# Order of the q and k products in the level stage of a hybrid decoder block, and the place of its operand region

## What is computed

```
b = jnp.cumsum(gi, axis=-2)
decay = jnp.where(causal, jnp.exp(jnp.where(causal, diff, 0.0)), 0.0)   # diff = b_i - b_j
attn = jnp.einsum('bhid,bhjd,bhijd->bhij', qi, ki, decay)
intra = jnp.einsum('bhij,bhje->bhie', attn, vi)
```

## Time and profile before

| | us |
|---|---|
| median of 3 runs | 1651.62 |
| lowest, highest | 1650.98, 1652.35 |
| the profiled execution, its own time | 1652.26 |
| its span, first to last instruction | 1650.5 |

### The profile page before, as it was taken

How to read it: one execution, slowest core, us unless ns; L and a number is a source line. 1 busy time by engine, 2 the same in 40 slices (tenths; PEclk the granted TensorE clock), 3 DMA queues, 4 the chain that set the end, 5 groups by cost and what they waited for, 6 DMA issues and landing times.

```text
span 1650.5 us, 29297 instructions
## 1 busy us (share of the span) xinstructions
PE 1622.8 (98%) x11680; PEld 1520.2 (92%) x11680; DVE 1120.8 (68%) x1276; ACT 820.9 (50%) x1076; POOL 6.0 (0%) x11
## 2 busy tenths in 40 slices
PE   7999999999899999999999999999999999999998
PEld 7999999879899999999888999999999999888886
DVE  5887767886667786877756677777777655644444
ACT  5567776556544633433446444444544544434332
POOL 0000000000000000000000000000000000000000
PEclk9999999999999999999999999999999999999999
DMA  9999978874368887877864777777776656555553
GB/s 369 346 320 335 314 253 258 279 250 135 108 231 279 287 277 234 284 250 260 316 211 131 228 239 228 229 230 233 237 230 214 190 180 204 178 189 193 179 192 138
DMA packets 190647, 389.46 MB, mean 236 GB/s; under 512 B 18386, under 2 KB 31058, under 8 KB 189794
## 3 DMA queue, kind: packets, MB, share of 16 engines
q1 hardware_dynamic: 185666, 370.40, 67.4%
q10 hardware_dynamic: 4898, 17.90, 3.3%
HBM read 386.16 MB, written 2.10 MB: 235 GB/s over the span
## 4 chain that ended last, share of the span: by engine, by line
PE 91%; DVE 4%; ACT 3%; issue 1%; DMA 0%; DVEq 0%; ACTq 0%
PE ps L589 20%; PE ps L593 20%; PE ps L591 20%; PE ps L616 8%; PE ps L618 8%; PE ps L617 8%; DVE w_lo L1407 2%; PE ps L541 1%; ACT w_hi L987 1%; PE ps L732 1%; DMA x_tok<-in_x 0%; PE ps L792 0%; DVE q_gla L1608 0%; PE ps L700 0%; PE ps L814 0%
## 5 line engine op out<-in xcount | busy, mean ns | idle before, releaser
L1407 DVE TENSOR_TENSOR w_lo<-raw,w_hi 128x1024 fp32r<-128x1024 f32 x530 | 626.0, 1222 | 474.3 <-ACT w_hi L987 474.0
L987 ACT ACTIVATE w_hi<-raw 128x1024 fp32r<-128x1024 f32 x530 | 532.7, 1052 | 662.8 <-PE ps L593 427.5
L589 PE MATMUL ps<-h2t,w_hi 128*128 128x256 f32 x1408 | 395.4, 281 | 0.7 <-DVE h2t L1826 0.7
L593 PE MATMUL ps<-h2t,w_lo 128*128 128x256 f32 x1408 | 393.0, 279 | 0.0
L591 PE MATMUL ps<-h2t,w_hi 128*128 128x256 f32 x1408 | 393.0, 279 | 0.0
L589 PE MATMUL ps<-ht,w_hi 128*128 128x256 f32 x1104 | 313.4, 284 | 0.0
L593 PE MATMUL ps<-ht,w_lo 128*128 128x256 f32 x1104 | 309.5, 280 | 0.0
L591 PE MATMUL ps<-ht,w_hi 128*128 128x256 f32 x1104 | 309.2, 280 | 0.0
L589 PEld LDWEIGHTS ps<-h2t,w_hi 128*128 128x128 f32 x1408 | 264.3, 188 | 0.9 <-issue 0.9
L593 PEld LDWEIGHTS ps<-h2t,w_lo 128*128 128x128 f32 x1408 | 264.8, 188 | 0.0
L591 PEld LDWEIGHTS ps<-h2t,w_hi 128*128 128x128 f32 x1408 | 263.4, 187 | 0.0
(11 more groups left out here) (283 smaller groups left out, 2003.2 us busy)
## 6 DMA issues: line engine op xcount, KB each, us to landing
raw<-in_w_ffn_up SPq DMA_DIRECT2D x176, 512.0 KB, 4.4
raw<-in_w_in SPq DMA_DIRECT2D x168, 512.0 KB, 4.8
ada<-in_w_ada SPq DMA_DIRECT2D x148, 512.0 KB, 6.5
raw<-in_w_ffn_down SPq DMA_DIRECT2D x88, 512.0 KB, 4.4
raw<-in_w_branch_b SPq DMA_DIRECT2D x32, 512.0 KB, 4.9
raw<-in_w_mix_out SPq DMA_DIRECT2D x32, 512.0 KB, 5.1
ada<-in_w_ada ACTq DMA_DIRECT2D x32, 512.0 KB, 4.0
raw<-in_w_branch_a SPq DMA_DIRECT2D x16, 512.0 KB, 5.2
```

The costliest lines, as they stand in the source:

```text
L589: mm(o, w_hi[:, s, k, cols], moving[:, kt, 0], start=opens, stop=False, skip_group_check=True)
L593: ins = mm(o, w_lo[:, s, k, cols], moving[:, kt, 0], start=False, stop=stop, skip_group_check=True)
L987: A(w_hi[:, slot], raw[:, slot], ACT.Copy).then_inc(hi_done, 1)
L1407: V.tensor_tensor(w_lo[:, slot], raw[:, slot], w_hi[:, slot].bitcast(F32), ALU.subtract)\
```

## The change

On VectorE the q and k products of `widen(lv)` go to the top of the step, in front of the low parts; the product of `dec` becomes a function of its own, `join_blocks(lv)`, and stays where `widen` was. On ScalarE `operands(1)` goes from the front of its step to behind the high parts, where the other levels' copies are. In the memory of each partition a tensor of 1920 bytes that nothing reads or writes, `spacer`, stands behind `masks`, so that all that follows, the operand region included, moves by 1920 bytes.

```diff
         masks = sb("masks", [P, LEVELS, P], U8)
+        spacer = sb("spacer", [P, 2048 - P], U8)
         cos_t = sb("cos_t", [P, S], F32)
...
                 if k == GLA + 1:
                     decays()
-                    operands(1)
...
                     if k == GLA:
                         gate_log()
-                    if 2 <= k - GLA < LEVELS - 1:
+                    if 1 <= k - GLA < LEVELS - 1:
                         operands(k - GLA)
...
                 V.tensor_tensor(q, q, spread(first, q), ALU.mult).then_inc(scaled, 1)
                 V.tensor_tensor(k, k, spread(second, k), ALU.mult).then_inc(scaled, 1)
-                if lv < LEVELS - 1:
-                    dve.wait_ge(scaled, scaled_at(lv))
-                    V.tensor_tensor(first, first, second, ALU.mult).then_inc(scaled, 1)
+
+            def join_blocks(lv):
+
+                first, second = (v[:, :, 0:1] for v in halves(dec, 1 << (lv - 2)))
+                dve.wait_ge(scaled, scaled_at(lv))
+                V.tensor_tensor(first, first, second, ALU.mult).then_inc(scaled, 1)
...
                 if k == GLA + 1:
                     first_scale(1)
+                if 2 <= k - GLA < LEVELS:
+                    widen(k - GLA)
                 if kind == "mix" and last:
...
                 if k == GLA + 1:
                     first_scale(0)
-                if 2 <= k - GLA < LEVELS:
-                    widen(k - GLA)
+                if 2 <= k - GLA < LEVELS - 1:
+                    join_blocks(k - GLA)
```

## The result

| | before | after |
|---|---|---|
| median, us (4 runs each, same chip) | 1651.98 | 1598.86 |
| lowest to highest | 1650.98 to 1652.82 | 1598.34 to 1603.16 |
| the profiled execution, its span | 1652.26, 1650.5 | 1598.98, 1597.2 |

The ratio is 0.9684, 95% interval 0.9667 to 0.9702: 53 us faster, where 11 were forecast and the range ended at 1638. The direction was right, the size wrong by five times.

A forecast was written before the change was run, and what follows sets the result against it. TensorE, 98% busy, was taken as the bound, losing time waiting for ScalarE's copies. Waits 9.2 plus clock 1.7, taken as 11.1 with the count by steps, gave 1652.26 - 11.1 = 1641.2; adjusted towards the median, 1641.0 us, range 1638 to 1646.

The forecast's parts named there:

- What bounds the kernel: Whole kernel: TensorE, busy 98%; only its waits or slow running can be won, 11.2 us lost in the level stretch.
- the loop: Level steps: score products wait 9.2 us for ScalarE's copies, which wait for VectorE's k product, queued behind low parts.
- the order of the products: VectorE, level steps: q and k products moved ahead of the low parts fit into its idle time; cost 0.
- the copies: ScalarE, level steps: copies finish 2.9 us before TensorE asks for them, so its waits go; gain 9.2 us.
- the clock: TensorE, 426.27 to 429.68: the half-clock stretch after the 3.02 us wait disappears; 1.7 us of products regained.
- The first step: ScalarE, first step: operands(1) behind the high parts delays copies 1.6 us, hidden by 3.9 us of slack; cost 0.
- The spacer: Partition memory: moving the operand region by 1920 bytes costs 0, with bounds of about 0.7% either way, 11 us.
- D: Operand region's new place changes TensorE's reads: slower, 1657 us at 1%, chance 0.09; gaining form 1633 us, chance 0.04.
- A: Level stretch: only the 9.2 us of waits go, not the half-clock loss; 1642.4, up to 1643.1 us; chance 0.16.
- B: Level steps: the wait stays in part under another name; 1647 us if half the pieces stay; chance 0.04.
- C: Level stretch: no change, TensorE waited for something else or gives the gain back later; about 1651.5 us; chance 0.03.
- What would show it: Changed trace: copy waits gone or under 1 us, 7.44 us steps, half-clock stretch gone, product times of 281, 279, 279 ns unchanged.

The follow-up runs named there:

- e2: Kernel after without the spacer (new order alone, operand region back at 960 modulo 2048); 1641.65 us, ratio to before 0.9936.
- e1: Kernel before with the spacer alone, instruction order unchanged; 1609.81 us, ratio to before 0.9739.
- f3: Kernel after with a spacer of 896 bytes: operand region at 1856, distance from w_hi 1344 modulo 2048; 1597.78 us.
- i3: Kernel after with w_hi at the slow distance (192 modulo 256) and w_lo at the quick one (64), region still at 832; 1625.49 us.
- f2: Kernel after with a spacer of 1792 bytes: operand region at 704, distance 448 (192 modulo 256); 1641.57 us.
- f4: Kernel after with a spacer of 192 bytes: operand region at 1152, the same place as w_hi modulo 2048, distance 0; 1649.75 us.
- e3: Kernel after with the 1920 bytes in front of raw instead: weights and region move together, region at 832, distance 192 as in before; 1642.15 us.
- f1: Kernel after with 128 bytes more in front of w_hi: weights at 1280, region back at 960, distance 320 as in after; 1602.54 us.
- g4: Kernel after with hid alone 64 bytes further on, its distance to w_hi 0 modulo 256; 1597.03 us, ratio to before 0.9667.
- h1: Kernel after with w_lo alone 128 bytes further on, at the slow distance (192 modulo 256), w_hi and region unmoved; 1599.92 us.

## Why the prediction was right and wrong

*What bounds the kernel; the loop; the order of the products; the copies; the clock.* Right, shown by e2: 1641.65, its profiled execution 1641.17, where 1641.0 and 1641.2 were forecast (the half way point of the working is 1640.9, a slip of 0.1). The steps of 7.44 us came, the copies were done at T + 4.6 (4.5 forecast), the products of level 3 ended just in front of the low parts (by 0.7 us, 0.8 forecast), and the half-clock stretch is gone. That the wait of 3.02 us brings this stretch on is borne out by e1, which kept both, and by e2 and after, which have neither; other stretches at half clock stayed or moved from execution to execution.

*The first step.* Right: in after the high parts begin at 389.95, ahead of the copies, and level 1 has no wait.

*The spacer.* The step that failed. It was priced at 0, with bounds of 0.7% from "reading 2 ns of 280 as sensitivity"; it was worth 43 us, 2.6%. The mechanism was among the rivals, D in its gaining form ("960 being the bad place"), with a chance of 0.04 and 8 us. Three errors made it so small.

The two rows taken as proof of insensitivity, L593 and L591 with their moving operands 1024 bytes apart, could not show any: f3 gives the same products at distances 320 and 1344, both 64 modulo 256. 1024 bytes is four whole periods. Every operand begins a whole number of 1024 bytes behind the start of the region, and every slice of w_hi at one of 512: by the layout all 256-column products of the kernel before had the same remainder, 192. Equal rows then mean that nothing was varied, not that nothing depends on it.

The bound was taken from the size of the noise in a duration, and durations overlap. 117.8 ns between starts was to be had from the trace of before, and products of 128 columns at L792, though in another format, follow each other there at 112 ns. No row says how short a 256-column product can be; with 112 as the floor, an estimate, 5.8 ns of 117.8 in some 8800 products are 51 us of room in which a gain could be. That was a bound to state, in place of 11.

The rule of 16 bytes a line (the Trainium skill, "SBUF — State Buffer", Specifications (TRN2), the row on cachelines), taken alone, would have made every shift of a multiple of 16 free. All shifts here are multiples of 32 and their times range from 1597.5 to 1650.3. The measurement decides.

*The rivals.* A, that only the waits of 9.2 us go: the stretch of the levels became 11.07 us shorter in the profiled execution of e2, so there the clock's part was in the gain. The times can't tell it from the forecast: e2's four runs reach from 1641.17 to 1643.30, and A said up to 1643.1. That execution ran longer at half clock elsewhere (870.5 to 877.4, where the one of before had 883.7 to 887.1), in sums and filler products ahead of the transposes of the feed-forward layer, and nothing of it was seen in the time: from the last level on both took 1181.4 us. B and C fell with the trace: no wait for the copies is left. D in its losing form had the sign wrong; in its gaining form it was right in kind and five times too small.

*What would show it.* "If they change by 2 ns or more, the spacer is no mere spacer" was the right sentence to have: they changed by 3 to 4.

## What to carry to other kernels

When TensorE is at 98%, look at the distance between its starts and not only at its gaps: here 112 us without a gap held 953 products in one kernel and 990 in the other. Where each kind of product streams from one tensor and loads from another, try their distance in steps of 32 or 64 bytes over 256; here it was worth four times the reordering and cost one line. A row that "shows no dependence" is worth something only if the quantity was varied in it, modulo every period that the layout hides.

## What the runs showed of the hardware

The distance between the starts of the products of this kernel (two operands in 4-byte elements, one loaded, one streamed) goes, nearly everywhere, by the distance of their places in the partition modulo 256 bytes, counted as weights less region: for 256 columns 113.4 to 113.6 ns at 64, 117.6 to 117.8 at 192, 118.3 to 118.7 at 32, 96 and 128, 119.9 at 0; for 512 columns 226.7 at 0, 228.9 at 64, 232.4 at 128, 233.3 or 233.4 at 32, 96 and 192. Distances of 160 and 224 were not run.

For 256 columns there are distinct rhythms, 113.3 and 117.8 ns at 64 and, seldom, at 192, and 113.3 and 118.9 in i3. A stretch keeps the one it has until something else passes through TensorE: a single `pace` product turned it to quick in after (885.4), to slow in f2 (905.7), and both ways in i3.

The instructions of VectorE and ScalarE that read and write the weights don't change with it: the low parts took 1221 or 1222 ns in before, after, f2, f3 and f4, the high parts 1051 to 1053.

Open: the mechanism. That the load of the next weights and the stream of the product before it get into each other's way fits a dependence on distance and not on place (e3, f1), and on the operands of the product (g4). But in its simple form, each load paying for itself, it fails for 256 columns: in h1 the loads of w_lo at the slow distance cost nothing, and in i3 whole passes are quick with two loads of three at it. Why a rhythm holds, and why a small product turns it, is not known, and no run had one of the two reads without the other.
